# Moving the activation buffers of a two-layer encoder by 32 bytes in SBUF

## The chip, the cores and the metric

The kernel runs on one core of a Trainium2 chip. The metric is the device time of one execution in microseconds. A profiled execution gives the trace; the other executions give only a time.

## What is computed

The program is a hybrid encoder of two layers over 256 tokens with 1024 features, all in float32. Cut to what matters here, each layer does:

```
h = rmsnorm(x) * (1 + sc1) + sh1
z = h @ w_in                      # 1024 x 4096 (even) or 1024 x 5120 (odd)
mixed = mixers(z) @ w_out         # recurrence + attention, or attention + pooling; 1024 x 1024
x = x + g1 * mixed
h = rmsnorm(x) * (1 + sc2) + sh2
gate, val = split(h @ w_up)       # 1024 x 5632
x = x + g2 * ((silu(conv3(gate)) * val) @ w_down)   # 2816 x 1024
```

The modulation vectors (sc, sh, g) come from a product of one conditioning vector with 1024 x 6144 weights in each layer. A last rmsnorm ends it. All weights are read once, some 170 MB in all.

## The kernel before

**Split products.** A float32 product is made of three matmuls in the format F32R. Weights and activations are each split in two halves: `hi` is the value rounded to F32R, `lo` the rest. The helper `three` (L1205 to L1210) issues `w_hi x h_hi`, `w_hi x h_lo` and `w_lo x h_hi` into one PSUM accumulator; every one of these matmuls stands at line L1208 in the trace:

```python
for n, (a, b) in enumerate(((w[0], h[0]), (w[0], h[1]), (w[1], h[0]))):
    lhsT, rhs = (b, a) if swap else (a, b)
    ins = pe.matmul(dst, lhsT, rhs, start=start and n == 0, stop=stop and n == 2, skip_group_check=True)
```

In the profile's names, `acc<-h_hi,w_hi` is a matmul that streams 256 columns of `h_hi` past a stationary 128x128 block of `w_hi`. The load of the stationary block is an instruction of its own (PEld, LDWEIGHTS) that goes on beside the matmul ahead of it. In units whose output is token-major (`swap`), the roles are turned round: the activation is stationary and the weights stream (`acc<-w_hi,h_hi`).

**The stream of weights.** The weights come in 110 units of 1 MB (128 partitions x 2048 floats). SyncE issues two DMAs for each into one of four slots of `w_raw`; ScalarE writes the unit's `hi` half (L532), VectorE its `lo` half (L808), each into one of two slots of `w_hi` and `w_lo`; TensorE takes 48 matmuls for a unit. The order is written out by hand on every engine and held together by semaphores. Units 0 to 15 are the even projection, 16 to 19 its output product, 20 to 41 the first up product, 42 to 52 the first down product, 53 to 72 and 73 to 76 the odd layer's projections, 77 to 98 and 99 to 109 the second feed-forward part. Between them lie the recurrence and the attention, which use matmuls of plain float32.

**Where the buffers lie.** `sb` puts one tensor after another in each partition, every size rounded up to 64 bytes, from a start that is a multiple of 64 (L139 to L150). `at_w` (L157) is the address of `w_hi`; `w_lo` lies 16 KB behind. Every tensor up to `consts` has a size that is a multiple of 256 bytes, so the weights' halves, `mod_acc`, `xT`, `work` and `consts` all lie at `at_w` plus a multiple of 256. Some small tensors follow. The line that is changed, L178, then moves the next address so that `h_hi` lies at a chosen distance from `at_w`, modulo 256:

```python
place[0] += (192 - (place[0] - at_w)) % 256
h_at = place[0]
h_hi = sb("h_hi", [P, KT, T], F32R)
h_lo = sb("h_lo", [P, KT, T], F32R)
arena = place[0]
```

`h_hi` and `h_lo` are 8 KB each. Behind them the `arena` of 69 KB holds by fixed offsets of whole KB nearly all that the stages share: the projections' results (`ze`, `zo`), the hidden layer's halves (`hid_hi`, `hid_lo`), the scores, the wrapped halves (`wrap_hi`, `wrap_lo`), `squared`, the first modulation tiles (`ada_first`), `late_raw`, `cs_low` and the output (`y_tok`). Without L178 the distance would be 64 with these sizes, so the line puts 128 bytes of padding in. A weight block starts at a multiple of 512 bytes in its slot, an activation tile at a multiple of 512 bytes in its buffer; the distance modulo 256 is thus one and the same for every split matmul.

Of the kernel before, what the change touches and what calls it, by code (L numbers as in the profile page):

```python
# [134 lines left out]
def encoder(nc, x, c, ada_w, ada_b, norm_mix_g, norm_ffn_g, even_w_in, even_w_out, hgrn_lb_logits, hgrn_norm_g,  # L135
            na_rpb, odd_w_in, odd_w_out, pool_w, pool_scale, ffn_w_up, ffn_conv_w, ffn_conv_b, ffn_w_down,
            final_norm_g, consts_in, out):
    with ExitStack() as ctx:
        place = [(nc.sbuf_base + 63) // 64 * 64]  # L139
# [17 lines left out]
        at_w = place[0]  # L157
# [17 lines left out]
        pstat = sb("pstat", [P, 4, 3, 2])  # L175
        poolw = sb("poolw", [P, 4, P])

        place[0] += (192 - (place[0] - at_w)) % 256  # L178
        h_at = place[0]
        h_hi = sb("h_hi", [P, KT, T], F32R)  # L180
        h_lo = sb("h_lo", [P, KT, T], F32R)
# [1549 lines left out]
```

## Time and profile before

| | us |
|---|---|
| median of 3 runs | 821.06 |
| the runs | 825.01, 819.38, 821.06 |
| the profiled execution | 819.27 |
| its span, first to last instruction | 817.6 |
| TensorE busy | 740.6 (91%) |
| mean granted clock of TensorE | 0.967 |

The span leaves out some 1.7 us of the execution's time. A matmul's busy time in the rows is its passage from its first column to its last result, and matmuls overlap: what a sequence of them costs is read from the distance of their starts, called pitch in this document.

### The profile page before, as it was taken

How to read it: one execution, taken by the hardware profiler on the slowest of the kernel's cores; microseconds unless marked ns; L12 is line 12 of the kernel's file. 1: busy time of each engine (PE TensorE's matmuls, PEld its weight loads, DVE VectorE, ACT ScalarE, POOL GpSimd, SP SyncE). 2: the span in 40 equal slices, each digit the busy share in tenths (PEclk: the TensorE clock that was granted, in tenths of full speed). 3: DMA queues.
4: the chain of work that ended last, by engine and by line, in shares of the span. 5: the costliest groups of instructions: out<-in, count | busy, mean ns of one | idle time of the engine just before them, and what ended most of it. 6: DMA issues, size and time to landing. Idle time of an engine off the chain costs nothing.

```text
span 817.6 us, 16825 instructions
## 1 busy us (share of the span) xinstructions
PE 740.6 (91%) x6601; PEld 712.3 (87%) x6601; DVE 583.4 (71%) x788; ACT 420.7 (51%) x655; POOL 84.4 (10%) x96
## 2 busy tenths in 40 slices
PE   3299998468789999999997999999998999999997
PEld 3299997257689999999997999998788999999997
DVE  3876777988768999876646678975547788886442
ACT  4244446451445676663324546555636666666332
POOL 0111114301000111000001002700003100000001
PEclk9699999799989999999997999999998999999999
DMA  9989887230157999857583897765134888865511
GB/s 357 368 246 328 302 302 254 88 105 2 54 154 210 297 283 286 276 189 282 180 300 112 275 338 239 232 232 180 53 84 119 237 236 247 236 219 196 182 44 52
DMA packets 160339, 171.23 MB, mean 209 GB/s; under 512 B 5210, under 2 KB 142371, under 8 KB 159267
## 3 DMA queue, kind: packets, MB, share of 16 engines
q1 hardware_dynamic: 152803, 143.30, 55.6%
q0 software_dynamic: 7488, 27.27, 9.2%
q8 instruction: 33, 0.54, 0.3%
q14 instruction: 15, 0.12, 0.0%
HBM read 169.49 MB, written 1.05 MB: 209 GB/s over the span
## 4 chain that ended last, share of the span: by engine, by line
PE 65%; DVE 8%; ACT 3%; issue 2%; DMA 1%; POOL 0%; SPq 0%; DVEq 0%; ACTq 0%; POOLq 0%
PE acc L1208 47%; PE big L1208 11%; DVE w_lo L808 3%; DVE qk L317 2%; ACT w_hi L532 1%; DMA w_raw<-in_odd_w_in 1%; DVE o_rms L1025 1%; PE big L1576 1%; PE big L1326 1%; PE aux L1276 1%; PE acc L1326 1%; PE big L1481 0%; PE aux L1599 0%; PE big L1563 0%; ACT zo L739 0%
## 5 line engine op out<-in xcount | busy, mean ns | idle before, releaser
L1208 PE MATMUL acc<-h_hi,w_hi 128*128 128x256 f32 x1248 | 353.1, 283 | 15.8 <-DVE h_lo L864 8.2
L1208 PE MATMUL acc<-h_lo,w_hi 128*128 128x256 f32 x1248 | 349.2, 280 | 0.0
L1208 PE MATMUL acc<-h_hi,w_lo 128*128 128x256 f32 x1248 | 348.9, 280 | 0.0
L808 DVE TENSOR_TENSOR w_lo<-w_raw,w_hi 128x1024 fp32r<-128x1024 f32 x220 | 266.8, 1237 | 104.5 <-ACT w_hi L532 104.4
L532 ACT ACTIVATE w_hi<-w_raw 128x1024 fp32r<-128x1024 f32 x220 | 224.7, 1050 | 92.0 <-PE acc L1208 70.9
L1208 PEld LDWEIGHTS acc<-h_hi,w_hi 128*128 128x128 f32 x1248 | 238.3, 191 | 18.8 <-issue 13.4
L1208 PEld LDWEIGHTS acc<-h_lo,w_hi 128*128 128x128 f32 x1248 | 238.5, 191 | 0.7 <-issue 0.5
L1208 PEld LDWEIGHTS acc<-h_hi,w_lo 128*128 128x128 f32 x1248 | 237.9, 191 | 0.0
L1208 PE MATMUL big<-hid_hi,w_hi 128*128 (+1 forms) x308 | 85.6, 278 | 0.0
L1208 PE MATMUL big<-hid_lo,w_hi 128*128 (+1 forms) x308 | 85.2, 277 | 0.0
L1208 PE MATMUL big<-hid_hi,w_lo 128*128 (+1 forms) x308 | 85.2, 276 | 0.0
L818 DVE SCALAR_TENSOR_TENSOR mod_acc<-ada_raw,cact,mod_acc 128x1024 f32<-128x1024 f32 x48 | 62.2, 1295 | 8.4 <-DMA ada_raw<-in_ada_w 8.2
L1208 PEld LDWEIGHTS big<-hid_hi,w_hi 128*128 128x128 f32 x308 | 57.9, 188 | 0.5 <-issue 0.4
L1208 PEld LDWEIGHTS big<-hid_lo,w_hi 128*128 128x128 f32 x308 | 57.8, 188 | 0.0
L1208 PEld LDWEIGHTS big<-hid_hi,w_lo 128*128 128x128 f32 x308 | 57.8, 188 | 0.0
L685 ACT ACTIVATE conv<-acc,vecs 128x256 f32<-128x256 f32 x44 | 24.8, 564 | 64.1 <-PE acc L1208 63.7
L435 POOL DMA_DIRECT2D ada_raw<-in_ada_w x44 | 23.5, 534 | 260.8 <-DVE mod_acc L818 260.8
L1090 DVE SCALAR_TENSOR_TENSOR conv<-acc,vecs,conv 128x255 f32<-128x255 f32 x44 | 21.2, 483 | 33.1 <-ACT conv L685 31.1
L1208 PE MATMUL acc<-w_hi,h_hi 128*128 128x256 f32 x144 | 40.6, 282 | 0.4 <-DVE w_lo L808 0.4
L1208 PE MATMUL acc<-w_lo,h_hi 128*128 128x256 f32 x144 | 40.1, 278 | 0.0
L1208 PE MATMUL acc<-w_hi,h_lo 128*128 128x256 f32 x144 | 40.1, 278 | 0.0
L584 ACT ACTIVATE ze<-acc 128x512 f32 (+1 forms) x16 | 9.6, 597 | 47.3 <-PE acc L1208 47.3
(225 smaller groups left out, 910.8 us busy)
## 6 DMA issues: line engine op xcount, KB each, us to landing
w_raw<-in_ffn_w_up SPq DMA_DIRECT2D x88, 512.0 KB, 5.1
ada_raw<-in_ada_w POOLq DMA_DIRECT2D x52, 512.0 KB, 5.7
w_raw<-in_ffn_w_down SPq DMA_DIRECT2D x44, 512.0 KB, 4.1
w_raw<-in_odd_w_in SPq DMA_DIRECT2D x40, 512.0 KB, 6.1
w_raw<-in_even_w_in SPq DMA_DIRECT2D x32, 512.0 KB, 5.9
ada_raw<-in_ada_w SPq DMA_DIRECT2D x22, 512.0 KB, 4.6
ada_first<-in_ada_w SPq DMA_DIRECT2D x5, 1024.0 KB, 8.1
w_raw<-in_even_w_out SPq DMA_DIRECT2D x8, 512.0 KB, 4.9
```

The lines of the kernel that those rows point to most:

```text
L317: return eng.tensor_tensor(to, to, total.unsqueeze(3).to_broadcast([P, 2, half // (2 * h), h]), ALU.mult)
L435: pool.dma_start(ada_raw[:, slot, :], src.rearrange("k p n -> p (k n)")).then_inc(ada_landed[slot], 16)
L532: nc.scalar.activation(w_hi[:, n % SPLIT, part], w_raw[:, n % RAW, part], ACT.Copy).then_inc(s_hi, 1)
L584: nc.scalar.activation(to, acc[:, (n - first) % 2, :], ACT.Copy, scale=scale).then_inc(z_evicted, 1)
L685: nc.scalar.activation(conv[:, a, :], acc[:, a, 0:T], ACT.Identity, bias=vecs[:, bass.ds(i * 4 + (V_CB + l * FT + u), 1)], scale=vecs[:, b ...
L808: dve.tensor_tensor(w_lo[:, n % SPLIT, part], w_raw[:, n % RAW, part], w_hi[:, n % SPLIT, part].bitcast(F32), ALU.subtract).then_inc(s_lo, 1)
L818: dve.scalar_tensor_tensor(out=sums, in0=ada_raw[:, slot, :], scalar=cact[:, bass.ds(k, 1)], in1=sums, op0=ALU.mult, op1=ALU.add).then_inc ...
L1025: link(dve.reciprocal(o_rms[:, part], o_rms[:, part]))
L1090: dve.scalar_tensor_tensor(out=conv[:, a, 1:T], in0=acc[:, a, 0:T - 1], scalar=tap(0), in1=conv[:, a, 1:T], op0=ALU.mult, op1=ALU.add).the ...
L1208: ins = pe.matmul(dst, lhsT, rhs, start=start and n == 0, stop=stop and n == 2, skip_group_check=True)
L1276: ins = pe.matmul(aux[:, 0, t:t + 1], squared[idx][:, k, t * P:(t + 1) * P], mean_w[:, 0:1], start=first and t == 0, stop=last, skip_group ...
L1326: ins = pe.matmul(bank[0:count, 0:P], pick, mod_acc[:, blocks[g] * P:(blocks[g] + 1) * P], start=g == 0, stop=g == count - 1, skip_group_c ...
```

## The change

The constant in L178 goes from 192 to 224. `h_hi`, `h_lo` and the whole arena lie 32 bytes higher; everything ahead of them stays. No instruction is added, removed or moved.

```diff
@@ -175,7 +175,7 @@
         pstat = sb("pstat", [P, 4, 3, 2])
         poolw = sb("poolw", [P, 4, P])
 
-        place[0] += (192 - (place[0] - at_w)) % 256
+        place[0] += (224 - (place[0] - at_w)) % 256
         h_at = place[0]
         h_hi = sb("h_hi", [P, KT, T], F32R)
         h_lo = sb("h_lo", [P, KT, T], F32R)
```

## Rows read from the trace of the kernel before

**Rows 1.** The page: span, and busy time by engine (share of the span, instructions).

```profile
span 817.6 us, 16825 instructions
...
PE 740.6 (91%) x6601; PEld 712.3 (87%) x6601; DVE 583.4 (71%) x788; ACT 420.7 (51%) x655; POOL 84.4 (10%) x96
```

**Rows 2.** The page: chain that ended last, by engine and by line.

```profile
PE 65%; DVE 8%; ACT 3%; issue 2%; DMA 1%; POOL 0%; SPq 0%; DVEq 0%; ACTq 0%; POOLq 0%
PE acc L1208 47%; PE big L1208 11%; DVE w_lo L808 3%; DVE qk L317 2%; ACT w_hi L532 1%; DMA w_raw<-in_odd_w_in 1%; DVE o_rms L1025 1%; PE big L1576 1%; PE big L1326 1%; PE aux L1276 1%; PE acc L1326 1%; PE big L1481 0%; PE aux L1599 0%; PE big L1563 0%; ACT zo L739 0%
```

**Rows 3.** Windows by stage: busy us and instructions by engine, clock, DMA.

```profile
core 0: us, PE busy (x) PEld busy (x) DVE busy (x) ACT busy (x) POOL busy (x), PEclk, DMA share, GB/s
0.00:42.00 42.00, 15.01 (x80) 12.24 (x81) 25.56 (x22) 15.56 (x27) 4.35 (x7) 0.84 0.97 357
42.00:137.00 95.00, 93.83 (x779) 91.03 (x780) 67.38 (x73) 46.74 (x57) 11.42 (x21) 1.00 0.91 297
...
244.00:411.00 167.00, 167.00 (x1474) 167.00 (x1474) 138.75 (x179) 98.48 (x141) 11.62 (x22) 1.00 0.76 245
...
442.00:600.00 158.00, 153.85 (x1395) 145.09 (x1394) 106.57 (x136) 82.67 (x142) 19.92 (x11) 1.00 0.64 207
...
627.00:793.00 166.00, 166.00 (x1466) 165.90 (x1464) 117.11 (x158) 96.83 (x139) 12.93 (x16) 1.00 0.65 202
```

**Rows 4.** Timeline of PE, 300 to 320 us (start, duration), 179 rows.

```profile
start us, us, engine line op out<-in xcount [idle before <-releaser]
299.79 0.28 PE L1208 MATMUL acc<-h_hi,w_hi 128*128 128x256 f32 x1
...
319.96 0.28 PE L1208 MATMUL acc<-h_lo,w_hi 128*128 128x256 f32 x1
```

**Rows 5.** Timeline of PE, 450 to 470 us, 172 rows.

```profile
449.82 0.28 PE L1208 MATMUL acc<-h_hi,w_lo 128*128 128x256 f32 x1
...
469.96 0.28 PE L1208 MATMUL acc<-h_hi,w_lo 128*128 128x256 f32 x1
```

**Rows 6.** L1208 in seven stretches: count, min/median/max ns, first and last start.

```profile
L1208 PE MATMUL acc<-h_hi,w_lo x346: 276/276/276, 244.9 to 362.2; 128*128 128x256 f32 x173
...
L1208 PE MATMUL acc<-h_hi,w_lo x88: 281/281/281, 442.7 to 473.5; 128*128 128x256 f32 x88
...
L1208 PE MATMUL acc<-h_hi,w_lo x29: 276/276/276, 100.3 to 109.8; 128*128 128x256 f32 x29
...
L1208 PE MATMUL acc<-h_hi,w_lo x31: 281/281/281, 113.4 to 124.0; 128*128 128x256 f32 x31
...
L1208 PE MATMUL acc<-w_lo,h_hi x9: 276/276/276, 75.1 to 77.9; 128*128 128x256 f32 x9
...
L1208 PE MATMUL acc<-w_lo,h_hi x31: 279/279/279, 125.4 to 136.0; 128*128 128x256 f32 x31
...
L1208 PE MATMUL big<-hid_hi,w_lo x14: 281/281/281, 801.0 to 805.6; 128*128 128x256 f32 x14
```

**Rows 7.** Timeline of PE at the end: output turning, 24 matmuls from first to last.

```profile
806.66 0.39 PE L1687 MATMUL acc<-work,xT 128*128 128x128 f32 x2
...
809.35 0.39 PE L1687 MATMUL big<-work,xT 128*128 128x128 f32 x2
```

**Rows 8.** Timeline of PE: 48 matmuls of 128 columns, weight loads of 24.

```profile
591.74 5.42 PE L1326 MATMUL big<-mod_acc,consts 128*24 128x128 f32 x48
597.09 0.66 PE L1576 MATMUL big<-zo,cpt 128*128 128x64 f32 x4
```

**Rows 9.** VectorE groups: the same operation on tiles ahead of and behind the gap.

```profile
L1156 DVE TENSOR_REDUCE stat<-mod_acc 128x1 f32<-128x384 f32 x8 | 4.4, 553 | 0.3
L1156 DVE TENSOR_REDUCE stat<-cs_low 128x1 f32<-128x384 f32 x8 | 4.4, 553 | 0.3
```

**Rows 10.** DMA issues: count, KB each, median us from issue to landing.

```profile
ada_raw<-in_ada_w SPq DMA_DIRECT2D x22, 512.0 KB, 4.6
...
late_raw<-in_ada_w SPq DMA_DIRECT2D x6, 512.0 KB, 5.6
```


## The prediction

> **What bounds the kernel now.** I read the page first: TensorE is busy for 740.6 of 817.6 us [rows 1]. The chain of waits that ended last is TensorE's for 65%, and 58% of the span, 47 and 11, belongs to the split matmuls of L1208 [rows 2]. The windows by stage say where TensorE alone sets the time: in the two feed-forward stages, 244 to 411 and 627 to 793 us, it is busy for 167.0 of 167 and 166.0 of 166 us, while VectorE, the next, is busy for 138.75 and 117.11 us and the DMA engines are at 0.76 and 0.65 [rows 3]. Those stages hold 1,474 and 1,466 matmuls. From 42 to 137 us it is nearly so (93.83 of 95), from 442 to 600 us it is broken by short waits (153.85 of 158), and the first 42 us belong to the DMA engines, which are at 0.97 there [rows 3]. So a change of what one split matmul costs would show nearly in full in some 330 us, in part in another 250.
>
> The change touches nothing but addresses. The question is thus whether the time of an instruction depends on them, and the view for that is the timeline of TensorE, read for the pitch. It shows two paces at full clock, of the same shape and tiles. From 299.79 to 319.96 us lie 178 pitches, 20.17 us / 178 = 113.3 ns [rows 4]. From 449.82 to 469.96 us lie 171, 20.14 us / 171 = 117.8 ns [rows 5]. I call them the fast and the slow pace. They can be told apart by the duration too, 276 ns against 281 (279 to 280 where weights stream) [rows 6]. A stretch keeps its pace: all 346 matmuls of a kind from 245 to 411 us are at 276 with equal minimum and maximum, all 88 from 443 to 474 us at 281 [rows 6]. The pace is mostly set where the stream starts again after a wait.
>
> Counting the pitches of L1208 down the timeline at full clock, from 40.9 to 806.3 us, and leaving out those with a wait in them, I find about 3,890 at the fast pace and 1,140 at the slow one. The slow ones lie at 86 to 97, 113 to 136, 208 to 221, 423 to 428, 442 to 491, 494 to 506, 551 to 580, 600 to 605 and 801 to 806 us.
>
> **The change part by part.** Nothing is removed, added or moved, and no wait changes, so the sum has three terms, each a change of the price of work that stays.
>
> First, the pitch of the split matmuls. Two things in the trace speak for no dependence. The two units of 100 to 110 us and the two of 113 to 124 us have the same shape and addresses modulo 256, and the first go at 276 ns, the second at 281 [rows 6]: the distance of 192 gives both paces. And where the roles are turned, the streamed operand lies at -192, that is 64, from the stationary one; such units go at the fast pace at 75 to 78 us and at the slow one at 125 to 136 us [rows 6]. So 192 and 64 give the same two paces. A distance of 224, or 32 with the roles turned, isn't in the trace, and 32 bytes is a finer step than any that it compares. The bounds are the nearest rows. Below: the 24 matmuls of plain float32 from 806.66 to 809.35 us, each with a full weight load, take 2.69 us / 24 = 112.1 ns [rows 7]; the 48 with 24-column loads from 591.74 to 597.09 us take 5.35 us / 48 = 111.5 ns with both their ends counted [rows 8]. Above: the slow pace, 117.8 ns. I take 113.3 and 117.8 as they are mixed now, since two distances share them, and keep both ends for the range.
>
> [...]
>
> Second, the operations of the other engines on the moved tiles. VectorE's maximum over 384 columns takes 553 ns on `mod_acc`, which lies at distance 0, and 553 ns on `cs_low`, at 192 [rows 9]. So a tile's place modulo 256 changes nothing there, at steps of 64 bytes. Were VectorE a few per cent slower on moved tiles, it would be covered in the feed-forward stages by the 28 and 49 us in which it is idle [rows 3]; without that cover, a per cent of its 583.4 us would be 5.8 us. I take 0, and up to 1 us for the attention and recurrence (137 to 205 us), where VectorE is busy for longer than TensorE's share of the chain covers.
>
> [...]
>
> Third, the DMAs into and out of the arena. A tile of 512 KB takes 4.6 us to land in `ada_raw`, at distance 0, and 5.6 us in `late_raw`, at 192 [rows 10]; the two are issued at different loads, so the 1.0 us is a bound and no measurement. The start, where five first modulation tiles of 1 MB land in the arena, is the only stage that waits for such transfers as a stream. I take 0, between -1 and +1 us.
>
> The sum is 0, or 819.27 us for the profiled execution; by the median, which lies 1.8 us above it, 821.
>
> **The rivals.** *The slow pace becomes the rule.* With 224 the streams lie 32 bytes from coinciding modulo 256 instead of 64, and if the slow pace is a collision of the reads of weights and activations, less distance could leave no start of a stream that escapes it. Price: 3,890 x 4.5 ns = 17.5 us, of which the 2,930 matmuls of the feed-forward stages pay in full (13.2 us) and I count half of the others (2.2 us): 15 us, 836 us by the median. For it: the two paces exist, and something sets them. Against it: 64 and 192 show no difference. It decides over 1% from the point at which some 1,850 of the 3,890 fast matmuls have gone over, that is if more than one of the two feed-forward stages does. *One long stretch goes over by chance.* The pace is kept once it is set, so one feed-forward stage of 1,470 matmuls that starts slow costs 6.6 us, giving 828; the range of the three runs, 5.6 us, would suit such a switch. *The collisions go away.* All matmuls come down to 112 ns: 3,890 x 1.3 + 1,140 x 5.8 = 5.1 + 6.6 = 11.7 us, and by the share of L1208 that lies in the chain (58% of 817.6 = 474 us, of some 5,280 x 113.5 ns = 600 us) 9.2 us, so 812 us. For it: a pitch near 112 exists. Against it: that pitch belongs to plain float32, which may have another limit. *The change does nothing that it says.* Were the padding absorbed elsewhere, nothing would move; but every size behind L178 is a whole number of KB, so the distance does change for all split matmuls, and this case gives the time of the forecast.
>
> **How the numbers follow.** No change in the paces 0.46 (821 us, 817 to 825), one stretch over by chance 0.05 (828), slow pace as the rule 0.32 (836), collisions gone 0.17 (812, not below 809). The predicted time is 821. The range goes from 809 to 838: the lower end is the whole of 11.7 us off the median, the upper one the 15 us and the 1 us of the second and the third term. One per cent, 8.2 us, is about what a measurement of this kernel can tell from no change. Faster by more than that: 0.15, since the case "collisions gone" clears it narrowly. Slower by more: 0.31, nearly all of the slow case. Within: 0.54.
>
> **What would show it.** If I am right, the timeline of the changed kernel has pitches of 113.3 and 117.8 ns at full clock in about the present shares, the feed-forward stages are 167 and 166 us long, and durations are 276 and 281 ns. If the slow pace is the rule, the feed-forward stages show 281 ns throughout and each is 6 to 7 us longer. If the collisions go, a third pitch at or under 112 ns appears. The second term would show in the means of VectorE's and ScalarE's groups on `h_lo`, `hid_lo` and `h_hi`, the third in the length of the first 42 us. The prediction is wrong if a pitch appears that the trace of before doesn't have, above all one over 118 ns, or if the pace after a restart is drawn otherwise than now.

## The result and the profile after

The changed kernel takes 839.39 us (median of 4 runs, 838.68 to 839.88), the kernel before beside it 823.03 us (4 runs, 819.38 to 833.86). The ratio is 1.0196, with a 95% interval from 1.0137 to 1.0256: slower, by 1.4 to 2.6%. Medians in this document are over all runs of a kernel, while a ratio leaves out runs that lie more than 1.5% above the fastest run of the same kernel. The forecast of 821 us and its range of 809 to 838 us missed it; the rival "the slow pace becomes the rule", at 836 us, comes nearest. Note the spreads too: the changed kernel's runs lie within 1.2 us, those of before within 14.5.

The page of the changed kernel: span, busy time by engine, and the chain by engine and by line. It answers to [rows 1, 2].

```profile
span 837.0 us, 16825 instructions
...
PE 765.6 (91%) x6601; PEld 736.1 (88%) x6601; DVE 583.4 (70%) x788; ACT 420.6 (50%) x655; POOL 83.2 (10%) x96
...
PE 69%; DVE 6%; ACT 2%; DMA 1%; issue 1%; POOL 0%; DVEq 0%; SPq 0%; ACTq 0%; POOLq 0%
PE acc L1208 50%; PE big L1208 12%; DVE qk L317 2%; DVE w_lo L808 2%; ACT w_hi L532 1%; DMA w_raw<-in_odd_w_in 1%; DVE o_rms L1025 1%; PE big L1576 1%; PE big L1326 1%; PE big L1563 1%; PE aux L1276 1%; PE aux L1599 0%; PE acc L1326 0%; PE big L1481 0%; PE big L1579 0%
```

The span is 19.4 us longer. VectorE is busy for the same 583.4 us as before; TensorE is busy for 25.0 us more with the same 6,601 instructions, and its share of the chain has grown from 65% to 69%.

The windows of the changed kernel over the four stages that answer to those of [rows 3]:

```profile
core 0: us, PE busy (x) PEld busy (x) DVE busy (x) ACT busy (x) POOL busy (x), PEclk, DMA share, GB/s
41.00:138.00 97.00, 96.31 (x783) 93.52 (x784) 67.85 (x74) 47.01 (x57) 12.22 (x23) 1.00 0.89 292
...
250.00:424.00 174.00, 174.00 (x1472) 173.81 (x1471) 135.81 (x173) 97.07 (x138) 11.66 (x22) 1.00 0.73 237
...
451.00:610.00 159.00, 155.23 (x1395) 146.50 (x1394) 107.79 (x139) 82.92 (x143) 19.92 (x11) 1.00 0.62 206
...
639.00:811.00 172.00, 172.00 (x1454) 172.00 (x1454) 116.38 (x158) 96.26 (x137) 10.71 (x16) 1.00 0.63 195
```

The two feed-forward stages take some 174 and 173 us for what took 167 and 166: the windows hold 1,472 and 1,454 matmuls, where those of before held 1,474 and 1,466, and the 12 that the second lacks would be another 1.4 us. TensorE never idles in them, VectorE idles more than before. So no wait has come in; the same matmuls take longer. The clock isn't the reason either: it is granted in full, 1.00, in all four windows, as before.

The first and last row of TensorE's timeline from 300 to 320 us (171 rows), which answers to [rows 4, 5]:

```profile
299.80 0.28 PE L1208 MATMUL acc<-h_hi,w_hi 128*128 128x256 f32 x1
...
319.91 0.28 PE L1208 MATMUL acc<-h_hi,w_lo 128*128 128x256 f32 x1
```

That is 20.11 us / 170 = 118.3 ns, where the kernel before had 113.3 in this stage. The durations of L1208 in three stretches, which answer to [rows 6] (count, minimum/median/maximum, first and last start):

```profile
L1208 PE MATMUL acc<-h_hi,w_lo x341: 277/281/285, 251.0 to 371.7; 128*128 128x256 f32 x171
...
L1208 PE MATMUL acc<-h_hi,w_lo x29: 277/280/285, 100.9 to 110.9; 128*128 128x256 f32 x29
...
L1208 PE MATMUL acc<-h_hi,w_lo x29: 277/280/285, 114.9 to 124.8; 128*128 128x256 f32 x29
```

There are no longer two paces. The stretches of 101 and 115 us, of which one was fast and one slow in [rows 6], are alike, and within each of them the duration goes from 277 to 285 ns, where before a stretch had one value. The pitches of single matmuls go from 115 to 123 ns in a pattern that repeats, with 118.3 ns as its mean in every stretch in which the activations stream. The token-major units, where weights stream, have another mean. Their first and last row from 127 to 137 us (88 rows):

```profile
126.74 0.28 PE L1208 MATMUL acc<-w_hi,h_lo 128*128 128x256 f32 x1
...
136.89 0.28 PE L1208 MATMUL acc<-w_hi,h_lo 128*128 128x256 f32 x1
```

It is 10.15 us / 87 = 116.7 ns.

That accounts for the time. Down the timeline at full clock, without the pitches that have a wait in them, the 3,600 pitches on `h` tiles rose in the mean from 114.3 to 118.3 ns, the 1,046 on `hid` tiles from 113.8 to 118.3, and the 469 of the token-major units stayed at 116.7. 3,600 x 4.0 + 1,046 x 4.5 = 14.4 + 4.7 = 19.1 us, and the span grew by 19.4. That the two are so close is in part luck. Both traces hold the same 6,601 matmuls in the same order, so the start of each can be set against that of its counterpart: the lag grows by 7.9 us from 245 to 411 us of the old timeline and by 7.3 from 628 to 793, 15.2 in the feed-forward stages. The other 4.2 us are a net sum of pitches and waits: -0.5 us up to the first split matmul, +1.5 from there to 137 us, +0.5 to 205, +2.2 to 245, -1.8 from 411 to 448, +2.1 to 628 and +0.2 at the end. The parts of +2.2 and -1.8 nearly cancel. They lie in stages in which TensorE waits, for up to 3.3 us at a time, and its granted clock is 0.50 for a while, and the two traces differ in how long: 6.8 us before and 13.7 after between 205 and 251 us, 10.2 before and 6.8 after between 411 and 452.

### The profile page after: what moved, and what is told of

Read it like the earlier page. It is cut to its first block, busy times and chain, and to the rows that moved or that the text cites. A ratio compares the mean times of both kernels' runs of the same rounds, so it can differ in the third digit from the quotient of the medians.

```text
span 837.0 us, 16825 instructions
## 1 busy us (share of the span) xinstructions
PE 765.6 (91%) x6601; PEld 736.1 (88%) x6601; DVE 583.4 (70%) x788; ACT 420.6 (50%) x655; POOL 83.2 (10%) x96
## 4 chain that ended last, share of the span: by engine, by line
PE 69%; DVE 6%; ACT 2%; DMA 1%; issue 1%; POOL 0%; DVEq 0%; SPq 0%; ACTq 0%; POOLq 0%
PE acc L1208 50%; PE big L1208 12%; DVE qk L317 2%; DVE w_lo L808 2%; ACT w_hi L532 1%; DMA w_raw<-in_odd_w_in 1%; DVE o_rms L1025 1%; PE big L1576 1%; PE big L1326 1%; PE big L1563 1%; PE aux L1276 1%; PE aux L1599 0%; PE acc L1326 0%; PE big L1481 0%; PE big L1579 0%
## 5 line engine op out<-in xcount | busy, mean ns | idle before, releaser
L1208 PE MATMUL acc<-h_hi,w_hi 128*128 128x256 f32 x1248 | 358.9, 288 | 15.5 <-DVE h_lo L864 8.3
L1208 PE MATMUL acc<-h_lo,w_hi 128*128 128x256 f32 x1248 | 355.0, 284 | 0.0
L1208 PE MATMUL acc<-h_hi,w_lo 128*128 128x256 f32 x1248 | 354.9, 284 | 0.0
L1208 PEld LDWEIGHTS acc<-h_hi,w_hi 128*128 128x128 f32 x1248 | 240.3, 193 | 18.3 <-issue 13.3
L1208 PEld LDWEIGHTS acc<-h_lo,w_hi 128*128 128x128 f32 x1248 | 240.0, 192 | 0.7 <-issue 0.5
L1208 PEld LDWEIGHTS acc<-h_hi,w_lo 128*128 128x128 f32 x1248 | 239.8, 192 | 0.0
L1208 PE MATMUL big<-hid_hi,w_hi 128*128 (+1 forms) x308 | 87.0, 283 | 0.0
L1208 PE MATMUL big<-hid_hi,w_lo 128*128 (+1 forms) x308 | 86.6, 281 | 0.0
L1208 PE MATMUL big<-hid_lo,w_hi 128*128 (+1 forms) x308 | 86.4, 281 | 0.0
L1208 PEld LDWEIGHTS big<-hid_hi,w_hi 128*128 128x128 f32 x308 | 57.9, 188 | 0.5 <-issue 0.4
L1208 PEld LDWEIGHTS big<-hid_lo,w_hi 128*128 128x128 f32 x308 | 58.1, 189 | 0.0
L1208 PEld LDWEIGHTS big<-hid_hi,w_lo 128*128 128x128 f32 x308 | 58.0, 188 | 0.0
L1208 PE MATMUL acc<-w_hi,h_hi 128*128 128x256 f32 x144 | 40.7, 283 | 0.0
L1208 PE MATMUL acc<-w_hi,h_lo 128*128 128x256 f32 x144 | 40.2, 279 | 0.0
L1208 PE MATMUL acc<-w_lo,h_hi 128*128 128x256 f32 x144 | 40.2, 279 | 0.0
```

## The experiments

Two theories stood at first. A: the distance between the streamed and the stationary operand sets the pitch. B: the activations' own place does, since they no longer begin on a multiple of 64 bytes. All kernels below compute the whole reference. Times are medians in us; ratios are to the kernel before on the same chip, which took 825.5 beside the first three experiments and the distance of 160, 824.9 beside 64, 128 and 0, 825.5 beside 32, 448 and the last experiment, and 823.1 beside 96. A pitch is worked out from the first and last row of a timeline, whose count of rows is given.

**Everything moved by 32 bytes.**

```diff
-        place = [(nc.sbuf_base + 63) // 64 * 64]
+        place = [(nc.sbuf_base + 63) // 64 * 64 + 32]
```

> Every buffer, the weights' halves too, lies 32 bytes higher; the distance of 192 is that of before. Theory A (the distance between the streamed and the stationary operand sets the pitch of the split matmuls): 113.3 and 117.8 ns as before, feed-forward stages of 166 to 167 us where they start fast, 819 to 828 us. Theory B (the activations no longer begin on a 64-byte boundary, and the weights' place doesn't matter): 118.3 ns throughout, 839 us.

Measured: 826.05 (10 runs), ratio 0.9965 [0.9919, 1.0012]. Its profiled execution took 827.32; one of the ten runs took 1877.89 us, and nothing on record says why. The timeline's ends in the first feed-forward stage, 300 to 320 us (179 rows), and in the second, 700 to 720 us (172 rows):

```profile
299.74 0.28 PE L1208 MATMUL acc<-h_lo,w_hi 128*128 128x256 f32 x1
...
319.92 0.28 PE L1208 MATMUL acc<-h_hi,w_lo 128*128 128x256 f32 x1
...
699.82 0.28 PE L1208 MATMUL acc<-h_hi,w_lo 128*128 128x256 f32 x1
...
719.96 0.28 PE L1208 MATMUL acc<-h_hi,w_lo 128*128 128x256 f32 x1
```

The first stage goes at 20.18 / 178 = 113.4 ns, the second at 20.14 / 171 = 117.8. So a place 32 bytes off the multiple of 64, shared by the weights, shows no cost here, at 113.4 and 117.8 ns and a ratio of 0.9965: theory B as stated falls. The second stage also shows the rival "one long stretch goes over by chance" at work: 1,438 matmuls kept the slow pace there, 1,438 x 4.45 ns = 6.4 us.

**The distance of 224, made with the weights.** The two halves of the weights move up by 32 bytes, what follows by 64, so that the activations lie on a multiple of 64 again.

```diff
+        place[0] += 32
         at_w = place[0]
         w_hi = sb("w_hi", [P, SPLIT, UNIT], F32R)
         w_lo = sb("w_lo", [P, SPLIT, UNIT], F32R)
+        place[0] += 32
...
-        place[0] += (192 - (place[0] - at_w)) % 256
+        place[0] += (224 - (place[0] - at_w)) % 256
```

> The distance is 224 as in the changed kernel, but made by moving the weights' halves 32 bytes off a 64-byte boundary, while the activations and the arena lie on one. Theory A: 118.3 ns throughout, 839 us. Theory B: 113.3 and 117.8 ns, 819 to 828 us. A third outcome, a pitch that neither kernel has, would say that both places count.

Measured: 840.44 (4 runs, one of them 858.86), ratio 1.0182 [1.0094, 1.0270]. The timeline's ends, 300 to 320 us (172 rows; L1210 is before's L1208):

```profile
299.76 0.28 PE L1210 MATMUL acc<-h_lo,w_hi 128*128 128x256 f32 x1
...
319.99 0.28 PE L1210 MATMUL acc<-h_lo,w_hi 128*128 128x256 f32 x1
```

It is 20.23 / 171 = 118.3 ns: the changed kernel's pitch and time, with the activations back on a multiple of 64. Together with the first experiment this decides between the two for theory A.

**Only the normalized activations at 224.** The arena goes back to 192.

```diff
-        place[0] += (192 - (place[0] - at_w)) % 256
+        place[0] += (224 - (place[0] - at_w)) % 256
...
         h_lo = sb("h_lo", [P, KT, T], F32R)
+        place[0] += 224
         arena = place[0]
```

> Only the normalized activations (h_hi, h_lo) lie at 224; the arena, with the hidden layer's halves, is back at 192. Theories A and B alike: the projections and the up products (some 4,200 of the 5,280 split matmuls, 118 of each feed-forward stage's 167 us) go at 118.3 ns, the down products (some 1,060) can keep 113.3; each down stage of 48 us is 2.1 us shorter than in the changed kernel, 834 to 836 us. If the other tiles of the arena (DMA targets, tiles of VectorE and ScalarE) were the cause instead, the time would be that of before, 819 to 823 us.

Measured: 834.87 (4 runs), ratio 1.0126 [1.0056, 1.0196], within the 834 to 836 us expected. The ends of the up products, 300 to 320 us (171 rows), and of the down products, 380 to 400 us (179 rows; L1209 is L1208):

```profile
299.79 0.28 PE L1209 MATMUL acc<-h_hi,w_hi 128*128 128x256 f32 x1
...
319.91 0.28 PE L1209 MATMUL acc<-h_hi,w_lo 128*128 128x256 f32 x1
...
379.82 0.28 PE L1209 MATMUL acc<-hid_lo,w_hi 128*128 x1
...
399.99 0.28 PE L1209 MATMUL big<-hid_hi,w_lo 128*128 x1
```

The up products go at 20.12 / 170 = 118.4 ns, the down products, one after the other without a wait between them, at 20.17 / 178 = 113.3. The pitch follows the tile that is read, within 5 matmuls of the first on a `hid` tile, and the arena's other uses show no part in it: the up products' 118.4 ns are the changed kernel's 118.3, though the arena is back at 192.

**Other distances.** In each of these kernels only the constant of L178 differs: 160, 64, 128, 0, 32 and 96.

```diff
-        place[0] += (192 - (place[0] - at_w)) % 256
+        place[0] += (160 - (place[0] - at_w)) % 256
```

The distance of 160:

> The distance is 160, 32 bytes less than before, where the changed kernel has 32 bytes more. Theory A, if nearness to a multiple of 256 is what costs (224 is 32 bytes from it, 160 is 96): no slower than before, 810 to 823 us. Theory A with a period of 64 bytes, or theory B: as the changed kernel, 118.3 ns, 839 us.

Measured: 841.31, ratio 1.0195 [1.0127, 1.0263]. The ends in the two feed-forward stages, 300 to 320 (171 rows) and 700 to 720 us (172 rows), and then of a token-major stretch, 130 to 137 us (61 rows):

```profile
299.73 0.28 PE L1208 MATMUL acc<-h_hi,w_hi 128*128 128x256 f32 x1
...
319.90 0.28 PE L1208 MATMUL acc<-h_hi,w_lo 128*128 128x256 f32 x1
...
699.82 0.28 PE L1208 MATMUL acc<-h_lo,w_hi 128*128 128x256 f32 x1
...
719.89 0.28 PE L1208 MATMUL acc<-h_lo,w_hi 128*128 128x256 f32 x1
...
129.75 0.28 PE L1208 MATMUL acc<-w_lo,h_hi 128*128 128x256 f32 x1
...
136.95 0.28 PE L1208 MATMUL acc<-w_lo,h_hi 128*128 128x256 f32 x1
```

The stages give 118.6 and 117.4 ns: two paces again, but neither is fast, and the 810 to 823 us of theory A with nearness to 256 are missed. The token-major stretch gives 7.20 / 60 = 120.0 ns. This left a period of 64 (192 good, 160 and 224 bad) or one of 256. Hence the next three.

> The distance is 64 modulo 256, with no padding left by the line. Theory A64 (what counts is the distance modulo 64, since 192 is good and 224 and 160 are both bad): two paces of 113.3 and 117.8 ns as before, 819 to 829 us. Theory A256 (each distance modulo 256 has a pitch of its own): another time than before by over 1%.

> The distance is 128. Theory A64: 113.3 and 117.8 ns, 819 to 829 us. Theory A256: another pitch; farthest from a multiple of 256, it could be the first without the slow pace, 815 to 819 us.

> The distance is 0: weights and activations coincide modulo 256. Theory A64: 113.3 and 117.8 ns, 819 to 829 us. Theory A256, if nearness to a multiple of 256 costs: the slowest of all, 117.8 ns or over throughout, 836 us or more.

Measured: 839.34, ratio 1.0196 [1.0129, 1.0263], for 64; 843.58, ratio 1.0246 [1.0184, 1.0309], for 128; 848.92 (4 runs, one of them 882.37), ratio 1.0311 [1.0232, 1.0389], for 0. The ends at 64, in a token-major stretch from 130 to 137 us (64 rows) and from 300 to 320 us (172 rows):

```profile
129.82 0.28 PE L1208 MATMUL acc<-w_hi,h_lo 128*128 128x256 f32 x1
...
136.96 0.28 PE L1208 MATMUL acc<-w_hi,h_lo 128*128 128x256 f32 x1
...
299.75 0.28 PE L1208 MATMUL acc<-h_hi,w_hi 128*128 128x256 f32 x1
...
319.89 0.28 PE L1208 MATMUL acc<-h_hi,w_hi 128*128 128x256 f32 x1
```

At 128 (171 rows) and then at 0 (169 rows), 300 to 320 us:

```profile
299.76 0.28 PE L1208 MATMUL acc<-h_hi,w_hi 128*128 128x256 f32 x1
...
319.93 0.28 PE L1208 MATMUL acc<-h_hi,w_lo 128*128 128x256 f32 x1
```

```profile
299.81 0.28 PE L1208 MATMUL acc<-h_hi,w_lo 128*128 128x256 f32 x1
...
319.97 0.28 PE L1208 MATMUL acc<-h_hi,w_lo 128*128 128x256 f32 x1
```

At 64 the activations stream at 117.8 ns, but where the weights stream the pitch is 7.14 / 63 = 113.3. At 128 it is 118.6 and at 0 it is 120.0. The period of 64 falls. Coinciding places are the worst, as that expectation said, but the farthest (128) isn't the best, and 64 and 192 differ: sign matters. That the token-major units are fast at 64, where streamed minus stationary is -64, that is 192, made a sharper theory: the signed distance alone decides, whatever is streamed.

> The distance is 32. The changed kernel's token-major units (roles turned, so 32 from the stationary operand to the streamed one) went at 116.7 ns. If the pitch is a property of the signed distance alone, whatever is streamed: feature-major units go at 116.7 ns here and token-major ones at 118.3, as the changed kernel's the other way round; 5,000 x 3.4 ns over the fast pace, 4/5 of it on the path: 832 to 835 us. If nearness to 0 is what costs, it lies between the distances 0 (120.0 ns, 849 us) and 64 (117.8 ns, 839 us): 843 us or so.

> The distance is 96, the last of the eight steps of 32. With the distance of 160, the token-major units (roles turned: 96 from the stationary operand to the streamed one) went at 120.0 ns, the feature-major ones at 117.2 to 120.0. If the signed distance alone decides, the two forms change places: feature-major units at 120.0 ns and so a time like that of distance 0, 847 to 850 us; token-major ones at 117 to 119. If the form of the unit counts too, feature-major units stay at 117 to 119 and the time at 841 us.

Measured for 32: 835.03, ratio 1.0152 [1.0084, 1.0219]. The ends of a token-major stretch, 130 to 137 us (61 rows), and from 300 to 320 us (174 rows):

```profile
129.78 0.28 PE L1208 MATMUL acc<-w_hi,h_hi 128*128 128x256 f32 x1
...
136.89 0.28 PE L1208 MATMUL acc<-w_hi,h_hi 128*128 128x256 f32 x1
...
299.73 0.28 PE L1208 MATMUL acc<-h_hi,w_hi 128*128 128x256 f32 x1
...
319.92 0.28 PE L1208 MATMUL acc<-h_hi,w_lo 128*128 128x256 f32 x1
```

Measured for 96: 844.20, ratio 1.0255 [1.0181, 1.0329], less than the 847 to 850 that its expectation named; set matmul against matmul, the distance of 0 falls behind it by 4.7 us in the first 245 us and by nothing in the two feed-forward stages. The same two stretches (61 and 169 rows):

```profile
129.77 0.28 PE L1208 MATMUL acc<-w_lo,h_hi 128*128 128x256 f32 x1
...
136.89 0.28 PE L1208 MATMUL acc<-w_lo,h_hi 128*128 128x256 f32 x1
...
299.73 0.28 PE L1208 MATMUL acc<-h_lo,w_hi 128*128 128x256 f32 x1
...
319.88 0.28 PE L1208 MATMUL acc<-h_lo,w_hi 128*128 128x256 f32 x1
```

The forms change places as the theory says: at 32, features 116.7 and tokens 118.5 ns (118.3 over all 469 token-major pitches), where the changed kernel has 118.3 and 116.7; at 96, features 119.9 and tokens 118.7, elsewhere in that trace 117.3, where the distance of 160 had 117.4 or 118.6 and 120.0. Mean pitches of whole stretches by signed distance, streamed minus stationary, modulo 256 (where two are given, some stretches have one and some the other):

| distance | activations stream, ns | same distance with weights streaming, ns | median us |
|---|---|---|---|
| 0 | 120.0 | 120.0 | 848.92 |
| 32 | 116.7, at times 117.8 | 116.7 (the changed kernel) | 835.03 |
| 64 | 117.8, seldom 113.3 | 117.8, at times 113.3 (before) | 839.34 |
| 96 | 119.9 | 120.0 (at 160) | 844.20 |
| 128 | 118.6, seldom 120.0 | 118.7 | 843.58 |
| 160 | 117.4 or 118.6 | 117.3 or 118.7 (at 96) | 841.31 |
| 192 (before) | 113.3 or 117.8 | 113.3, at times 117.8 (at 64) | 823 to 826 |
| 224 (changed) | 118.3 | 118.3 (at 32) | 839.39 |

**A distance of 448.** It is 192 modulo 256, and another modulo 512.

```diff
         place[0] += (192 - (place[0] - at_w)) % 256
+        place[0] += 256
```

> The distance is 192 modulo 256 as before, but 448 instead of 192 modulo 512, by 256 bytes of padding more. If 256 is the period: 113.3 and 117.8 ns, 818 to 829 us. If the period is longer: another pitch, and a time of 835 us or more.

Measured: 821.27 (10 runs), ratio 0.9993 [0.9948, 1.0038]. The ends, 300 to 320 (172 rows) and 700 to 720 us (179 rows):

```profile
299.78 0.28 PE L1209 MATMUL acc<-h_hi,w_hi 128*128 128x256 f32 x1
...
319.92 0.28 PE L1209 MATMUL acc<-h_hi,w_hi 128*128 128x256 f32 x1
...
699.73 0.28 PE L1209 MATMUL acc<-h_hi,w_lo 128*128 128x256 f32 x1
...
719.90 0.28 PE L1209 MATMUL acc<-h_hi,w_hi 128*128 128x256 f32 x1
```

The paces are those of before, 117.8 and 113.3 ns; this time the first stage is the slow one, and the second is fast. The execution of this trace took 823.77 us. The shift by 256 leaves both paces as they are; those by 32 to 160 give the streams of activations the means of 116.7 to 120.0 ns in the table, with 113.3 left in a few stretches at 64.

**Only the lower halves of the activations at 224.** `h_lo` moves by 32 bytes (and with it the tiles of the recurrence that share its place); `h_hi` and the arena stay. Not shown are the two lines in which the offsets of those tiles rise by 32 too.

```diff
         h_hi = sb("h_hi", [P, KT, T], F32R)
+        place[0] += 32
         h_lo = sb("h_lo", [P, KT, T], F32R)
+        place[0] += 224
         arena = place[0]
...
```

> h_hi and the arena stay at 192; only h_lo, which one matmul in three of the projections and up products streams, lies at 224. If each matmul pays by its own pair: two pitches of three are as before and one is as in the changed kernel, (2 x 113.3 + 118.3) / 3 = 115.0 ns, and with some 4,200 such matmuls 5 us over before at equal paces. If the pace is one lock of the whole sequence: either all three stay at 113.3, or all go to 117 ns or more, 830 us and over. Down products keep 113.3 and 117.8.

Measured: 839.63 (4 runs), ratio 1.0196 [1.0132, 1.0260]. The ends, 300 to 320 us (170 rows):

```profile
299.81 0.28 PE L1210 MATMUL acc<-h_lo,w_hi 128*128 128x256 f32 x1
...
319.91 0.28 PE L1210 MATMUL acc<-h_hi,w_lo 128*128 128x256 f32 x1
```

It is 20.10 / 169 = 118.9 ns, not 115.0. Here one stream in three at 224 costs the whole sequence its fast pace, and even a little more than all three do (118.3 ns). The pitch isn't a sum of prices of single matmuls. The down products, at 192 on both sides, went on at 117.8 ns in the first stage (380 to 400 us), one of their two paces.

## Why the prediction was wrong

The view was right: the question was whether the pitch depends on the place, L1208's pitch was the term that carries the sum, and the feed-forward stages pay for it in full. The second term is 0 as predicted, and the third lies within its bounds of -1 and +1 us. For the second, VectorE is busy for the same 583.4 us, and its maximum takes the same time on moved and unmoved tiles in the changed kernel, as in [rows 9]:

```profile
L1156 DVE TENSOR_REDUCE stat<-cs_low 128x1 f32<-128x384 f32 x8 | 4.4, 553 | 0.3
L1156 DVE TENSOR_REDUCE stat<-mod_acc 128x1 f32<-128x384 f32 x8 | 4.4, 553 | 0.3
```

For the third, the first split matmul before and then in the changed kernel:

```profile
40.66 0.35 PE L1208 MATMUL acc<-h_hi,w_hi 128*128 128x256 f32 x1 [2.27 <-DVE h_lo L864]
...
40.13 0.36 PE L1208 MATMUL acc<-h_hi,w_hi 128*128 128x256 f32 x1 [2.27 <-DVE h_lo L864]
```

It starts at 40.13 us for 40.66, 0.53 us earlier.

The step that failed is the first term: "I take 113.3 and 117.8 as they are mixed now, since two distances share them". It rested on two readings. One was that the distance of 192 gives both paces, as the stretches at 100 and 113 us show. That is true (276 and 281 ns of duration at one distance), but it only says that the distance isn't the only thing that sets the pace; I read it as if the distance were nothing. The other was that the units with roles turned, at 64, have the same two values: of their 469 pitches at full clock in the trace of before, 117 are of 113 or 114 ns and 348 of 117 to 119. Both readings compare only 192 and 64, and the step from them to 224 had no row under it. At 224 the traces of the changed kernel and of the second experiment show one mean of 118.3 ns in place of 113.3 and 117.8, the sign that the prediction itself named for being wrong: a pitch over 118 ns that the trace of before doesn't have. Nor are 192 and 64 alike: with activations streaming at 64, both long stages go at 117.8 ns and only 171 of 4,612 pitches, 1 in 27, are of the fast pace's 113 or 114 ns. The trace of before gives a hint of that, since 348 of its 469 token-major pitches, which are at 64, were slow (117 to 119 ns) against 818 of the 4,674 others, but no safe one: in the first experiment, at the same distances, 206 of 469 token-major pitches were slow, 44%, and 1,873 of the 4,641 others, 40%. Two of eight steps were compared, and these happen to be the only two that have a fast pace at all. A third that coincides with neither, such as 0 (120.0) or 96 (119.9), would have shown the dependence, but no split matmul of the kernel before has one; the 24 matmuls of [rows 7] are at 0, but they are plain float32, whose 112.1 ns show nothing of it.

The rival had the place of the cost, the distance, and its first point right (224 has no fast pace: 118.3 ns throughout) and the size too small. I priced the slow pace at 117.8; at 224 it is 118.3, so that those of the 1,140 slow matmuls that stream activations pay 0.5 ns more too. And I counted half of what the matmuls outside the feed-forward stages cost as covered by waits, 2.2 us, where the net lag outside them is 4.2. So 15.2 us in the feed-forward stages instead of 13.2, and 4.2 outside: 19.4 instead of 15. The range's upper end of 838 hung on both. The rival's reason, nearness to 0, isn't right either: 32 is as near as 224 and faster (116.7 ns for 118.3; 835.03 us for 839.39), 160 is farther than 224 and no faster (841.31 us). The faster rival had nothing for it: in none of the twelve kernels with another layout has a stretch of split matmuls a mean under 113.3 ns.

The chance event is real within one execution, as the first experiment and the distance of 448 show. That it also spreads the runs of one kernel fits, but isn't shown, since no kernel was traced twice. The 40 runs of the kernel before that were timed beside the experiments go from 816.6 to 832 us, but for two of 841, and the distance of 448 spreads likewise (819.5 to 831.1 in 10 runs), while the kernels with no long stage at the fast pace stay within 1 to 6 us but for one run each of 858.86 and 882.37. A trace with one slow feed-forward stage (the first experiment) belongs to an execution of 827 us, one with none to 819; but the distance of 448, with one as well, took 824: set matmul against matmul, its trace is 3.6 us shorter than the first experiment's, and 2.7 us of that lie ahead of 245 us.

What stays open is the mechanism beneath. That the reads of the two operands disturb each other is my inference, and no run shows it. What the runs show is that the pitch goes with the distance: 118.3 ns at 224 whichever operand is moved, 113.4 and 117.8 with everything moved by 32 bytes, 113.3 and 117.8 at 448 as at 192. What chooses between 113.3 and 117.8 ns at a restart wasn't tried. Of steps finer than 32 bytes there is no result.

## What to carry to other kernels

In this kernel, where TensorE is busy for 91% of the span and every split matmul has a full weight load beside it, the places of the two operands relative to each other are a parameter that no instruction shows. With matmuls of 256 columns in F32R it is worth 3%, from 823 to 849 us; other formats and shapes weren't tried. So read the pitch of starts, not the busy time, compare it at all eight steps of 32 bytes, and pin it as this kernel does, for a new small tensor ahead of the activations moves it silently. All tiles that take part should be at the good distance, since one stream in three at 224 cost the whole gain in its stages (118.9 ns for 113.3). And a trace in which a parameter takes two of eight values says little of the other six, the more so when one of the two values gives two results.

## What the runs showed of the hardware that was not expected

- The mean pitch of 256-column F32R matmuls with a 128-column load beside each depends on the signed distance from the stationary to the streamed operand, modulo 256 bytes: 113.3 ns at best (192), 120.0 at worst (0). The values of the table don't ask which of the two is the weight.
- At 192, and more seldom at 64, the stream has two stable paces, 113.3 and 117.8 ns, and keeps the one it has for some 1,440 matmuls. When the tiles change to 192 without a wait between, the pitch changes within 5 matmuls: from 118.4 to 113.3 ns in the third experiment, from 118.9 to 117.8 in the last. Other distances have two means as well: 116.7 and 117.8 at 32, 117.4 and 118.6 at 160.
- A long stage of some 1,440 matmuls can thus take 6.4 us more or less at full clock with no wait in it, with the same layout (the first experiment, the distance of 448). That two executions of one program differ for this reason is likely, but no program was traced twice.
